# Gaps between the rounded weight tiles of a float32r decoder trunk, and a temporary that moves into dead memory

## The reference

```python
def sq_relu_mlp(h, w1, w2):
    u = jax.nn.relu(h @ w1)
    return (u * u) @ w2

def reference(x, ...):
    h = x
    for i in range(DEPTH):                       # DEPTH = 2
        hn = rms_norm(h, norm_mix_g[i])
        mix = pool_mixer(hn, ...) if i % 2 == 0 else ssd_mixer(hn, ...)
        h = h + mix
        h = h + sq_relu_mlp(rms_norm(h, norm_mlp_g[i]), mlp_w1[i], mlp_w2[i])
    return rms_norm(h, final_g)
```

## Time and profile before

| | |
|---|---|
| median of 3 runs | 1115.41 us (1114.95 to 1115.59) |
| the profiled execution: its own time | 1115.47 us |
| the profiled execution: span of its instructions | 1113.7 us |
| PE busy | 1093.4 us, 98% |
| DVE, ACT, POOL busy | 574.2, 464.2, 585.8 us |
| memory read | 114.32 MB |

### The profile page before, as it was taken

The page is one execution under the profiler, slowest core; times in us unless marked ns, Lnnn a source line. Parts: engine busy times, 40 slices in busy tenths (PEclk is TensorE's granted clock), DMA queues, the critical chain, the costliest instruction groups (busy, mean ns, idle before and its releaser), DMA issues.

```text
span 1113.7 us, 15232 instructions
## 1 busy us (share of the span) xinstructions
PE 1093.4 (98%) x5106; PEld 895.5 (80%) x5106; DVE 574.2 (52%) x648; ACT 464.2 (42%) x796; POOL 585.8 (53%) x442
## 2 busy tenths in 40 slices
PE   8999999999999999999999999999999999999996
PEld 6788888888888788787787778888888888888885
DVE  6756421455423384674876847666554124553213
ACT  7433222233333338557585675443342222333331
POOL 3666544445565635437364474656664444455551
PEclk9999999999999999999999999999999999999998
DMA  7222232222223325332433333222222222222221
GB/s 265 95 98 99 93 103 97 94 94 94 95 94 97 97 78 149 123 128 100 133 100 128 120 107 106 94 94 95 94 98 95 100 103 95 94 94 96 94 94 75
DMA packets 39428, 117.03 MB, mean 105 GB/s; under 512 B 4064, under 2 KB 10848, under 8 KB 39392
## 3 DMA queue, kind: packets, MB, share of 16 engines
q1 hardware_dynamic: 38960, 115.70, 31.0%
q10 hardware_dynamic: 432, 0.86, 0.2%
HBM read 114.32 MB, written 2.23 MB: 105 GB/s over the span
## 4 chain that ended last, share of the span: by engine, by line
PE 84%; ACT 6%; DVE 5%; issue 2%; DMA 1%; POOL 1%; DVEq 0%; SPq 0%; ACTq 0%
PE bank L745 27%; PE bank L747 27%; PE bank L746 26%; ACT m L560 1%; ACT w_hi L394 1%; DVE x_conv L1135 1%; PE bank L929 1%; DMA m<-acs_scratch 1%; PE bank L938 1%; DVE m L1215 1%; POOL w_lo L635 1%; DVE bank L1264 1%; PE bank L788 1%; PE bank L946 0%; DVE x_lo L1002 0%
## 5 line engine op out<-in xcount | busy, mean ns | idle before, releaser
L635 POOL TENSOR_TENSOR w_lo<-w_raw,w_hi 128x512 fp32r<-128x512 f32 x372 | 499.0, 1347 | 473.4 <-ACT w_hi L394 473.1
L394 ACT ACTIVATE w_hi<-w_raw 128x512 fp32r<-128x512 f32 x372 | 230.9, 626 | 400.4 <-PE bank L747 396.9
L745 PE MATMUL bank<-x_hi,w_hi 128*128 128x512 f32 x848 | 335.6, 396 | 2.7 <-DVE x_lo L1002 1.7
L747 PE MATMUL bank<-x_hi,w_lo 128*128 128x512 f32 x848 | 330.3, 389 | 0.0
L746 PE MATMUL bank<-x_lo,w_hi 128*128 128x512 f32 x848 | 330.1, 389 | 0.0
L745 PE MATMUL bank<-act_hi,w_hi 128*128 128x512 f32 x640 | 251.2, 392 | 0.0
L747 PE MATMUL bank<-act_hi,w_lo 128*128 128x512 f32 x640 | 249.0, 389 | 0.0
L746 PE MATMUL bank<-act_lo,w_hi 128*128 128x512 f32 x640 | 249.0, 389 | 0.0
L745 PEld LDWEIGHTS bank<-x_hi,w_hi 128*128 128x128 f32 x848 | 159.2, 188 | 40.0 <-issue 6.1
L746 PEld LDWEIGHTS bank<-x_lo,w_hi 128*128 128x128 f32 x848 | 159.2, 188 | 34.5 <-issue 2.2
L747 PEld LDWEIGHTS bank<-x_hi,w_lo 128*128 128x128 f32 x848 | 159.2, 188 | 33.4
(11 more groups left out here) (138 smaller groups left out, 671.2 us busy)
## 6 DMA issues: line engine op xcount, KB each, us to landing
w_raw<-weights SPq DMA_DIRECT2D x186, 512.0 KB, 3.3
m<-acs_scratch SPq DMA_DIRECT2D x16, 512.0 KB, 4.2
decay_in<-eacs_scratch SPq DMA_DIRECT2D x24, 128.0 KB, 3.7
x_token<-x_tok SPq DMA_DIRECT2D x4, 512.0 KB, 6.9
residual<-xt SPq DMA_DIRECT2D x8, 256.0 KB, 10.1
out_t<-scaled_residual SPq DMA_DIRECT2D x8, 256.0 KB, 2.4
pooling_matrices<-pooling ACTq DMA_DIRECT2D x1, 576.0 KB, 5.1
constants<-consts SPq DMA_DIRECT2D x1, 208.0 KB, 10.3
```

Of the source, the lines that this page charges most:

```text
L394: act.activation(whi[:, c % 2, part], raw[:, c % 2, part], ACT.Copy).then_inc(hi_ready, 1)
L635: pool.tensor_tensor(wlo[:, c % 2, part], raw[:, c % 2, part], whi_f[:, c % 2, part], ALU.subtract).then_inc(lo_ready, 1)
L745: pe.matmul(out, wh, xh, start=start, stop=False)
L747: return pe.matmul(out, wl, xh, start=False, stop=stop)
```

## The change

Each tile of `w_hi` gets 16 unused float32 values (64 bytes) behind it, each tile of `w_lo` 20 (80 bytes). The tile steps become 576 and 592 bytes in place of 512. ScalarE and GpSimd then write, and GpSimd reads, four pieces of 128 values where they had one run of 512 (`w_raw`, which the transfers fill, stays as it was). TensorE's operands keep their shape, 128 adjoining values per tile. The two tensors grow by 1024 and 1280 bytes in a partition. `y_tmp` no longer has memory of its own and lies on the second buffer of `tmp`. Everything behind `w_lo` moves up by 2304 bytes, and what stood behind `y_tmp` by 256. No instruction is added, removed or moved on any engine, no wait changes, and each engine's instructions stand in the order they had.

```diff
+HI_GAP, LO_GAP = 16, 20
...
-        whi, _ = sb("w_hi", [P, 2, 1024], F32R)
-        whi_f = whi[:, :, :].bitcast(F32)
-        wlo, _ = sb("w_lo", [P, 2, 1024], F32R)
+        whi, _ = sb("w_hi", [P, 2, 8, P + HI_GAP], F32R)
+        whi_f = whi[:, :, :, :].bitcast(F32)
+        wlo, _ = sb("w_lo", [P, 2, 8, P + LO_GAP], F32R)
...
-        tmp, _ = sb("tmp", [P, 2, TOK])
+        tmp, o_tmp = sb("tmp", [P, 2, TOK])
...
-        ytmp, _ = sb("y_tmp", [P, TOK])
+        ytmp, _ = sb("y_tmp", [P, TOK], F32, o_tmp + 4 * TOK)
...
                 part = slice(512 * half, 512 * half + 512)
-                act.activation(whi[:, c % 2, part], raw[:, c % 2, part], ACT.Copy).then_inc(hi_ready, 1)
+                act.activation(whi[:, c % 2, 4 * half:4 * half + 4, 0:P],
+                               raw[:, c % 2, part].rearrange("p (k n) -> p k n", k=4), ACT.Copy
+                               ).then_inc(hi_ready, 1)
...
                 part = slice(512 * half, 512 * half + 512)
-                pool.tensor_tensor(wlo[:, c % 2, part], raw[:, c % 2, part], whi_f[:, c % 2, part],
-                                   ALU.subtract).then_inc(lo_ready, 1)
+                tiles = slice(4 * half, 4 * half + 4)
+                pool.tensor_tensor(wlo[:, c % 2, tiles, 0:P], raw[:, c % 2, part].rearrange("p (k n) -> p k n", k=4),
+                                   whi_f[:, c % 2, tiles, 0:P], ALU.subtract).then_inc(lo_ready, 1)
...
-                    w = slice(P * k, P * k + P)
-                    last = three(out, whi[:, c % 2, w], wlo[:, c % 2, w], hi[:, tile0 + k, :],
+                    last = three(out, whi[:, c % 2, k, 0:P], wlo[:, c % 2, k, 0:P], hi[:, tile0 + k, :],
                                  lo[:, tile0 + k, :], start and k == 0, stop and k == 7)
```

More of the change, by code:

```diff
@@ L799, in pool_maps @@
                     for k in range(2):
-                        w = bass.ds(512 * (gi % 2) + 256 * mt + 128 * k, P)
-                        last = three(bank[2 * gi + mt][:, :], whi[:, gi // 2, w], wlo[:, gi // 2, w],
+                        i = 4 * (gi % 2) + 2 * mt + k
+                        last = three(bank[2 * gi + mt][:, :], whi[:, gi // 2, i, 0:P], wlo[:, gi // 2, i, 0:P],
                                      xhi[:, 2 * gi + k, :], xlo[:, 2 * gi + k, :], k == 0, k == 1)
@@ L847, in half_units @@
                         pe.wait_ge(ylo_ready, GT * g + k + 1)
-                        w = slice(P * (GT * half + k), P * (GT * half + k) + P)
-                        last = three(out, whi[:, (U_SSM + u) % 2, w], wlo[:, (U_SSM + u) % 2, w],
+                        i = GT * half + k
+                        last = three(out, whi[:, (U_SSM + u) % 2, i, 0:P], wlo[:, (U_SSM + u) % 2, i, 0:P],
                                      act_hi[:, GT * g + k, :], act_lo[:, GT * g + k, :], k == 0, k == GT - 1)
```

## The result

The changed kernel takes 1136.18 us (median of 4 runs, 1135.84 to 1136.52) where the kernel before takes 1115.19 us (also 4 runs). The ratio is 1.0188, 95% interval 1.0175 to 1.02: 21 us slower. The prediction was 1115.4 us with a range of 1092 to 1121, so it was wrong.

What follows compares the result with a forecast made beforehand. The prediction took the distance between TensorE's float32r matmul starts as the bound, 1012 us of the 1113.7 us span. All terms were put at 0, so 1115.47 + 0 gave 1115.4 us, with a range of 1092 to 1121.

Steps and rivals of the forecast that it cites:

- What bounds the kernel: Whole kernel: TensorE's 4464 float32r matmuls at 0.2267 us between starts make 1012 of the 1113.7 us span.
- The distance: Both MLPs, time between starts of float32r matmuls: stays at 0.2267 us despite the gaps, a term of 0.
- The second argument: Both MLPs: distance equal for all tiles and unmoved by ScalarE and GpSimd accesses, so no collision by address; term 0.
- The sign: Both MLPs: load and moving tile collide at equal places modulo 512 and the gaps part them; faster, chance 0.32.
- at most 52 us less: All 4464 float32r matmuls: full gain if each falls from 0.2267 to 0.215 us, 1063 us; chance 0.14 near it.
- a longer load: Weight loads of line 747, shifted `w_lo` tiles: a quarter longer, 235 ns, costs 12 us, 1127 us; chance 0.07.
- the direction "slower": Whole kernel: longer load, 0.07, plus ScalarE and GpSimd paying for the pieces, +3.1 us, 0.07; together 0.14.
- The 12 ns over bfloat16: Each float32r matmul takes about 12 ns more than a bfloat16 one; whether coinciding tile starts cause it was left open.
- ScalarE, GpSimd, `y_tmp`: Rounding and split in four pieces, and the shared temporary: each 0; upper end for the pieces +3.1 us, chance 0.07.
- The 0.3 us upper bound for GpSimd: GpSimd's split: three more pieces, priced by its smallest instruction of 102 ns, cost at most 0.3 us per instruction.
- The two rules beside the sum: Float32r matmuls, skill page: N / 2.4 + about 2.5 ns gives 49 us gain, 1067 us; independent read ports make gaps do nothing.

Runs made afterwards that it cites:

- run 4: The probe, a separate kernel of only float32r 512-column matmuls, varying the byte distance between weight and moving tile starts: 226.7 ns at 0 and 256, 233.3 at 64.
- run 1: Changed kernel without gaps, their 2304 bytes in one piece behind `w_lo`, shared temporary kept, against the kernel before: 1115.44 against 1115.77 us, ratio 0.9988.
- run 7: Separate kernel of matmul series with differences of 4 to 28 bytes, other start places and bfloat16: no float32r series below 226.7 ns, bfloat16 216 ns.

## Why the prediction was wrong

**What bounds the kernel: right.** The prediction took the distance between starts for the one quantity that matters, 1012 us of the span, and wrote that 1 ns of it is 4.5 us. The change worked through this alone: 5.6 ns, 25 us, less some waits.

**The distance: the step that failed.** "So I put this term at 0." It rested on two arguments. The first was that at the earlier trace rows a load at 64 and at 256 bytes left the distance at 0.23 us. The place at 256 bytes could not show anything: 256 is a whole period, 226.7 ns in the probe. The place at 64 bytes was one load after a long row at 0, and there the loss comes one matmul later. In run 4 the series with gaps of 64 and 80 bytes begins with distances of 227, 226, 226, 236 and 231 ns. The first load at 64 runs beside the third of these, which is untouched; the fourth pays. At 117.64 no float32r matmul of 512 columns followed that could have paid. (Not every place is like this: the series with a gap of 80 bytes alone begins with 227, 226, 227, 227 and 235, where the fifth is the one beside the first load at 80.) And the reading was too coarse for a loss in any case: the timeline gives hundredths of a microsecond, in which 226.7 and 233.3 ns are both 0.23, so it could rule out 0.215 and nothing on the slower side. To the nanosecond the two distances of the earlier trace rows are 226 and 228. At other such places of the same trace, ahead of the transposes of lines 897 and 888, they are 230 to 237 (237 at 437.17, where the view shows 0.23). Those loads start 256 bytes off and last 0.14 us, so the place modulo 256 doesn't explain them and the cause is open; but they show that a load of another kind can move the distance, and the prediction didn't look at them. The second argument was that the distance was the same for all tiles. It was, because every start was a multiple of 512 apart, two whole periods: an even distance under equal places says nothing of other places.

**The sign.** The prediction allowed for a collision only in the direction that the gaps would cure, "at most 52 us less", with the coincidence as the suspect. The runs show the reverse: for 512 columns and a full load no place is faster than coincidence modulo 256 bytes. The size of a gain was bounded, that of a loss never was; the slower side held only a longer load. That load was priced at 12 us and came out at 0: 188 ns as before. So the direction "slower", given 0.14, rested on the wrong mechanism too.

**The 12 ns over bfloat16.** Left as "the whole question". No shift that was tried removes them; the least mean of any series of 512 columns is 226.7 ns. With the full load at 0 they are the same for 256, 384 and 512 columns, but they change with the load's size and, at 256 columns, with its place (6.7 ns at 64 bytes). What makes them is open.

**ScalarE, GpSimd, `y_tmp`: right.** 626 and 1340 ns; run 1 shows the temporary and the move at nothing. The 0.3 us upper bound for GpSimd was not needed (the smallest GpSimd instruction before was of 99 ns, not 102, which changes nothing).

**The two rules beside the sum.** The Trainium skill's page "TensorE: Matmul & The Clock Gate" (Part 1, on 56 against 53.3 ns) has the rule by which 49 us were to be won, N / 2.4 + about 2.5 ns. The traces agree with it for bfloat16 (216 ns in run 7) and for no float32r series. The same page of the Trainium skill (Part 2, the load of the stationary operand) says that a load takes no read bandwidth from the running matmul. The prediction drew from it that the gaps do nothing, and that did not come true: 226.7 ns became 233.3 with nothing changed but the start of the loaded tile. Since the loss doesn't follow the load's size, the runs don't show whether it is bandwidth that is lost.

**What stays open.** What it is that repeats every 256 bytes, why a smaller load costs more at 0 and a little less at 64 and 128, why a mixed sequence costs more than its places, and why the distance at a place is not always the same. The runs show that the gaps cost 21 us by the place of the weight tiles against the moving ones, and the size of it for this shape; the mechanism below that they don't show.

## What to carry to other kernels

When a stream of float32r matmuls bounds a kernel, look at where the stationary and the moving tiles start modulo 256 bytes before anything else: here 512-column matmuls ran at 226.7 ns with both alike and at multiples of 32, and at 229 to 236 at most other places, and 64 bytes more ahead of the weights were enough to lose 2%. With 256 columns the better place was another, so this is to be measured for each shape. An even value in a trace is no proof that a quantity doesn't depend on the layout, if the layout never varied, and a difference of 7 ns is not seen in one distance that is read to 10 ns; a small kernel of series with one start moved at a time, 500 us long, gave in one run what the trace could not. And bound a disputed cost on both sides even where the story has only one.

## What was unexpected of the hardware

- The distance between 512-column float32r matmuls has a period of 256 bytes in the difference of the two starts: 226.7 ns at 0, 240 and 16, 229 at 192, 232 to 234 from 32 to 160, with the moving tile at a multiple of 32 bytes.
- Gaps in `w_lo`, one load in three, cost as much as gaps in `w_hi`, two in three (13 us each): the loss spreads to the matmuls around a shifted load.
- bfloat16 matmuls don't depend on it: 216 ns at 0, 64 and 128.
- With 256 moving columns 64 bytes is better than 0, 113.3 against 120 ns.
- Slowing TensorE by 25 us cost 21, mostly since two waits of about 2 us in the SSD mixer vanished.
